# Larger experts: the second pair's down weights fetched into idle scratch instead of the weight ring

## The reference, cut to what matters

```python
def expert_block(args):
    xi, e = args
    hid = jax.nn.silu(xi @ w1[e]) * (xi @ w3[e])
    return hid @ w2[e]
```

## Time and profile before

| | us |
|---|---|
| median of 3 runs | 2576.78 |
| lowest and highest | 2572.59, 2577.24 |
| the profiled execution | 2580.19 |
| its span in the profile | 2578.5 |
| TensorE busy | 2424.8 (94%) |
| VectorE busy | 674.2 (26%) |
| ScalarE busy | 450.8 (17%) |
| DMA | 769.64 MB, mean 298 GB/s |

### The profile page before, as it was taken

One profiled execution on the slowest core, in us unless ns is written; L12 is line 12 of the kernel. 1 busy time (PEld: TensorE's weight loads), 2 busy tenths in 40 slices (PEclk: granted clock), 3 DMA queues, 4 the chain that ended last, 5 costly groups with the idle time before them and its releaser, 6 DMA issues.

```text
span 2578.5 us, 28316 instructions
## 1 busy us (share of the span) xinstructions
PE 2424.8 (94%) x11460; PEld 1388.3 (54%) x11460; DVE 674.2 (26%) x1398; ACT 450.8 (17%) x816; POOL 0.2 (0%) x4
## 2 busy tenths in 40 slices
PE   7999999888888999998888899999999999999998
PEld 5776734333335684433333568884444778874443
DVE  2652331001012223110010244124111633142113
ACT  3141121000001112100000025103111233112111
POOL 0000000000000000000000000000000000000000
PEclk8999999999999899999999999999999999999999
DMA  9348669999998226999999842345999343158994
GB/s 403 139 151 366 269 271 429 429 428 428 429 428 347 98 90 242 428 429 428 428 429 428 349 145 97 126 163 231 420 425 420 142 146 111 66 215 336 428 424 177
DMA packets 53941, 769.64 MB, mean 298 GB/s; under 512 B 5984, under 2 KB 6496, under 8 KB 7008
## 3 DMA queue, kind: packets, MB, share of 16 engines
q1 hardware_dynamic: 53568, 768.17, 72.2%
q10 hardware_dynamic: 288, 0.26, 0.0%
HBM read 767.36 MB, written 1.05 MB: 298 GB/s over the span
## 4 chain that ended last, share of the span: by engine, by line
PE 72%; DMA 24%; DVE 2%; ACT 1%; issue 1%; SPq 0%; ACTq 0%; DVEq 0%
DMA slab<-in_experts 23%; PE psum L400 14%; PE psum L432 13%; PE psum L1933 9%; PE psum L1923 8%; PE psum L1970 7%; PE psum L1905 6%; PE psum L696 4%; PE psum L503 1%; DMA slab<-in_dense 1%; PE psum L1243 1%; PE psum L1956 1%; PE psum L746 1%; PE psum L626 0%; PE psum L1947 0%
## 5 line engine op out<-in xcount | busy, mean ns | idle before, releaser
L1923 PE MATMUL psum<-slab 128*64 128x512 f32 x2048 | 461.5, 597 | 77.1 <-DMA slab<-in_experts 73.8
L400 PE MATMUL psum<-slab 128*128 128x256 f32 (+5 forms) x1464 | 372.3, 412 | 5.2 <-DVE slab L1801 3.4
L1970 PE MATMUL psum<-slab 128*64 128x512 f32 x1536 | 357.8, 601 | 2.6 <-ACT slab L2001 2.6
L1923 PEld LDWEIGHTS psum<-slab 128*64 128x64 f32 x2048 | 142.4, 137 | 389.9 <-issue 273.6
L432 PE MATMUL psum<-slab 128*128 128x256 f32 x1504 | 338.9, 386 | 5.2 <-ACT slab L2158 2.3
L400 PEld LDWEIGHTS psum<-slab 128*128 128x128 f32 (+2 forms) x1464 | 261.8, 189 | 107.5 <-issue 69.1
L432 PEld LDWEIGHTS psum<-slab 128*128 128x128 f32 x1504 | 289.7, 193 | 52.6 <-issue 9.6
L1905 PE MATMUL psum<-slab 128*128 128x256 f32 x1024 | 249.3, 385 | 1.2 <-DVE slab L2023 1.2
L1933 PE MATMUL psum<-slab 128*64 128x512 f32 x1024 | 225.3, 592 | 0.0
L1905 PEld LDWEIGHTS psum<-slab 128*128 128x128 f32 x1024 | 183.2, 189 | 72.7 <-issue 50.3
L2013 DVE TENSOR_TENSOR slab<-psum,slab 128x512 f32<-128x512 f32 (+1 forms) x64 | 35.7, 558 | 691.5 <-PE psum L1923 502.2
(11 more groups left out here) (429 smaller groups left out, 1574.5 us busy)
## 6 DMA issues: line engine op xcount, KB each, us to landing
slab<-in_experts SPq DMA_DIRECT2D x288, 2048.0 KB, 20.2
slab<-in_dense SPq DMA_DIRECT2D x73, 2048.0 KB, 9.4
slab<-in_dense SPq DMA_DIRECT2D x2, 1680.0 KB, 17.9
slab<-in_vec SPq DMA_DIRECT2D x1, 2571.5 KB, 32.8
slab<-in_dense SPq DMA_DIRECT2D x1, 1328.0 KB, 27.4
slab<-in_dense SPq DMA_DIRECT2D x2, 640.0 KB, 14.6
slab<-in_xT SPq DMA_DIRECT2D x1, 1024.0 KB, 8.3
out<-slab SPq DMA_DIRECT2D x2, 512.0 KB, 2.6
```

The lines of the kernel that those rows point to most:

```text
L400: ins = mm(out_ap, lhs, rhs, start=(n == 0), stop=(n == len(pairs) - 1), skip_group_check=True)
L1923: ins = mm(psum[CAP * e:CAP * e + CAP, n, :], xg[:, k, CAP * e:CAP * e + CAP], sl(w, KD)[:, e * (KD // 2) + i, :], start=(k == 0), stop=(k ...
L1970: ins = mm(psum[CAP * e:CAP * e + CAP, 2 + half, :], hidT[:, f, CAP * e:CAP * e + CAP], w, start=(f == 0), stop=(f == fc - 1), skip_group_ ...
```

## The change

The down weights of pair 1, in both layers of the first model, no longer use ring slots. Their 16 blocks go to places in `hT` and the scratch area by five DMAs: three (2048, 2048 and 1536 columns, 11 blocks) are issued right behind the last fill of pass 0, without a wait; two (2048 and 512 columns, 5 blocks, into `order` and the head of `xN`) behind pass 1's four remaining fills and a wait on SP for all eight `sorted_done` of the layer. All five raise `constants_in`. Then pass 2 is issued in straight code, its first two fills into the slots that the first pair's down weights leave, and the loop on SP begins with pass 3. TensorE, ahead of the first down unit of pair 1, waits for `constants_in` in place of a slot, and takes no slot for either half. Units and their numbers are as before.

```diff
+        EARLY_DOWN = ((HO, 0, 0, 2048), (AO + 800 + 13824, 0, 2048, 2048), (AO + 800 + 15872, 1, 2048, 1536),
+                      (AO + 800 + 11776, 1, 0, 2048), (AO + 800 + 4608, 1, 3584, 512))
+
+        def early_down(w0, w1, late):
+
+            return [((w0, w1)[half][:, at:at + n], view(home, n))
+                    for home, half, at, n in (EARLY_DOWN[3:] if late else EARLY_DOWN[:3])]
+
+        def early_block(half, block):
+
+            for home, part, at, n in EARLY_DOWN:
+                if part == half and at <= 512 * block < at + n:
+                    return view(home + 512 * block - at, 512)
...
                 for f, u in zip(pass_fills(l, 0), free):
                     fill(f, first + u)
-                with sp.Fori(1, passes) as i:
+                if kind == 1:
+                    ahead = pass_fills(l, 1)
+                    for src, dst in early_down(ahead[4][0], ahead[5][0], False):
+                        sp.dma_start(dst, src).then_inc(sems["constants_in"], 16)
+                    for f, u in zip(ahead[0:4], free):
+                        fill(f, first + units + u)
+                    sp.wait_ge(sems["sorted_done"], KD * (l + 1))
+                    for src, dst in early_down(ahead[4][0], ahead[5][0], True):
+                        sp.dma_start(dst, src).then_inc(sems["constants_in"], 16)
+                    for f, u in zip(pass_fills(l, 2), free):
+                        fill(f, first + 2 * units + u)
+                with sp.Fori(3 if kind == 1 else 1, passes) as i:
...
             q.e.wait_ge(sems["hidT_ready"], q.due("hidT_ready"))
-            down = slot(q)
+            early = begin and kind == 1
+            if early:
+                q.e.wait_ge(sems["constants_in"], q.due("constants_in", 16 * len(EARLY_DOWN)))
+            down = None if early else slot(q)
             pe_down(kind, down, 0).then_inc(sems["unit_done"], 1)
...
-            if kind == 1:
+            if kind == 1 and not early:
                 down = slot(q)
             pe_down(kind, down, 1).then_inc(sems["unit_done"], 1)
...
-                    w = sl(down, KD)[:, 4 * e + f, :] if kind == 1 else sl(down, 4)[:, 2 * e + f, 512 * half:512 * half + 512]
+                    if down is None:
+                        w = early_block(half, 4 * e + f)
+                    elif kind == 1:
+                        w = sl(down, KD)[:, 4 * e + f, :]
+                    else:
+                        w = sl(down, 4)[:, 2 * e + f, 512 * half:512 * half + 512]
```

More of the change, by code:

```diff
@@ L389, in build @@
         A0 = PER + 288 + 2 * S
+        assert A0 == AO + 800
         def slot(q):
```

## The result

| | before | changed |
|---|---|---|
| median, us (4 runs each) | 2576.27 | 2560.22 |
| lowest, highest | 2572.59, 2577.24 | 2558.62, 2561.34 |
| ratio, 95% interval | | 0.994 (0.9923 to 0.9957) |
| profiled execution, span | 2580.19, 2578.5 | 2561.34, 2559.7 |

The change makes the kernel 16 us faster; 13 were forecast. The spans of the two profiles differ by 18.8 us, so the first question is how much of that belongs to the change.

The account below looks back on a forecast made before the run. Both larger-expert stages were taken as bound by DMA bytes; gains of 6.4 us (layer 0) and 6.5 us (layer 1) sum to 12.9, say 13 us, giving a median of 2563.8 us, range 2557 to 2571 us.

Parts of the forecast that it names:

- What bounds: Larger-expert stages of layers 0 and 1: both end when the bytes have come, with DMA saturated at 428 GB/s.
- ladder: Chain to each stage's end: a DMA piece of 25.5 us, then 16 matmuls of 3.7 us, repeating.
- (2): Ahead of the first pair: 11 early blocks, 2.88 MB, 6.7 us, lie wholly in idle DMA and cost nothing.
- (3): Behind the sort: 5 late blocks, 1.31 MB, 3.1 us, flow in the second idle stretch; the wait costs nothing.
- (4): Down product of pair 1: TensorE's single wait for all 16 blocks has 20 us of slack.
- (5): Start of pass 3, layer 1: full ring makes DMA rest 3.3 us, so pass 3 begins 6.5 us earlier, not 9.8.
- Layer 0: Larger-expert stage of layer 0, by the same steps as layer 1: gain 6.4 us.
- (6): End of both stages: still byte-bound, lead 6.5 us against 52 us deficit; layer 1's last-pair stop of 3.30 us follows.
- rival B: TensorE's stops move with code placement; two more outside byte-bound stretches take 6.6 us: 2570.4 us. Chance of bad case 0.08.
- Rival A: Both layers: the ring does not fill, so the whole 9.8 us per layer is gained: 2557.2 us. Chance 0.05.
- C: Lead does not reach the stages' end, or blocks miss the idle stretches: no difference, 2576.8 us. Chance 0.07.
- D: Pair 1 waits for down weights carried behind pass 2's fills, 15.1 us late: slower by 17.2 us, 2594.0 us. Chance 0.04.

Follow-up runs that it names:

- more scratch: Changed kernel, plus first half of pair 2's down weights moved to the scratch that pair 1's first half leaves: 2560.69 us, then 2560.64 us.

## Why the prediction was right, point by point

- **What bounds** (right). Both stages hang on the bytes: the ladder of landings runs up to the last pair but one in layer 1 in every profile, and up to the last pair in layer 0 in all but one (the second with more scratch, which stopped there). The waits of PE on landings fell: 35.2 us in 32 stops in the earlier trace rows, now 29.1 in 26 over the same stretch.
- **(2) and (3), the early and late blocks cost nothing** (right). They flow in the idle stretches (windows above), and the wait on the sort holds nothing up: pass 2's first fill is issued at 1007.15 us, 0.05 us behind the end of unit 5 (1003.45 + 3.65).
- **(4), no wait at pair 1** (right), and its price if it comes (right: 15.1 us were worked out, 13.7 measured, the whole kernel +18.0 for +17.2).
- **(5), the rest** (right in place and cause, its credit mis-sized). I gave 6.5 us in layer 1; the stage shows 7.5. The term that was mis-sized is the time from the end of a fill's bytes to its landing. I read 2.3 us from a fill deep in a long flow and let it stand for both kernels, so that it dropped out of the difference. SP's issue of pass 3's first fill, before and after, from the views of the two lines:

```profile
L355 SPq DMA_DIRECT2D slab<-in_experts x1: 332/332/332, 1051.7 to 1051.7; - x1
...
DMA to landing us min/median/max: 15.3/15.3/15.3
```

```profile
L380 SPq DMA_DIRECT2D slab<-in_experts x1: 343/343/343, 1040.1 to 1040.1; - x1
...
DMA to landing us min/median/max: 7.7/7.7/7.7
```

The fill landed at 1067.0 us before, as forecast (1060.0 + 4.9 + 2.3 = 1067.2), and at 1047.8 after, 1059.5 in the old frame, where the same lags give 1053.5 + 4.9 + 2.3 = 1060.7. So 7.5 us are won. From the end of unit 13 (1036.27 + 3.6 = 1039.9 us) 7.9 us pass to the landing, not 2.0 + 4.9 + 2.3 = 9.2. The start was as forecast: by the windows from 1041 to 1043 us (262 and 246 GB/s) the flow begins, in effect, at 1041.8 us, 1.9 behind the unit. The missing 1.2 us are in the last term: 1041.8 + 4.9 = 1046.7, landed 1047.8, so 1.1 instead of 2.3 us. The trace of the kernel before could have told me. Its own start from rest, the fill of 1019.0 us:

```profile
L355 SPq DMA_DIRECT2D slab<-in_experts x1: 333/333/333, 1019.0 to 1019.0; - x1
...
DMA to landing us min/median/max: 7.7/7.7/7.7
```

It landed at 1026.7 us, 1.0 behind the end of its bytes (1020.8 + 4.9); the delay of 2.3 us had built up later in the flow, and a rest takes it away.
- **Layer 0** (right in size, in part by luck): 6.4 us forecast, 6.3 measured with the same unit 5. The landing of pass 3's first fill is 7.3 us earlier there too (81.9 us behind the stage's first up product before, 74.6 in the third profile of the changed kernel, which has the same unit 5). So the term was mis-sized here as well; the total came out because a new delay took some 1 us back. By pass 3's fourth fill the lead is 6.5 us (96.6 and 90.1); it lands 5.6 us behind the third there, 6.2 in the first profile, where 4.9 are the bytes.
- **(6), the stop of 3.30 us stays** (right), **rival B** (wrong in its premise): it is there in all twelve profiles of these kernels, 3.1 to 3.9 us, at the end of layer 1's loop, though the code moved; in layer 0 it came once, in the second profile of the kernel with more scratch and not in the first. So where the code lies does not decide it alone: the same kernel showed the stop of layer 0 in one execution and not in the other. What causes it stays open. No further stop came in the changed kernel.
- **Rival A** failed by the rest, seen in the profile; **C** by the ladder; **D** did not occur in the changed kernel, and came true at its price once two DMAs stood later in SP's order.
- **The sum.** Stages 13.9 us for 12.9; the four medians, each beside the kernel before, give 16.1, 16.8, 13.5 and 15.9. The 2 us between are outside the stages and not explained. So the forecast of the median, 3.6 us above what was measured, misses 1 us by the term above, 2 by what lies outside the stages, and 0.5 since the median of before stands at 2576.27 us with its fourth run instead of 2576.78. The profiles' 18.8 holds 3 us more than the medians; the profiled execution of before had 5 us more between the stages than its repeat, of which some 3.4 are the lower clock's by the estimate above. For the same reason layer 1's first pair starts at 973.2 us in the profile and not at the 978 that I gave as a sign.

## What to carry to other kernels

Taking bytes off a saturated queue is worth only what the ring can take up: once all slots are full, the queue rests until TensorE frees the next one. Here six slots filled before TensorE had used one of the next pair, so of 9.8 us per layer 2.3 to 3.5 were given back, and the first half of the blocks had its whole price, the second less than half. Where an early transfer is placed matters only once the ring has room; work out the next full point before looking for more idle time. Read the lag of a landing where the queue has just started and again deep in its flow before using it as one number. And read a stage from its own two marks in several profiles: here a stretch that no edit touched moved by 5 us between two executions, a third of the change.

## What was not expected of the hardware

In a long flow the landings do not keep step with the bytes. In the changed kernel the fill issued at 1018.0 us landed at 1029.4, the next (1021.4) at 1035.8 us, 6.4 us later, and yet the bytes flowed at 431 GB/s from 1011 to 1038 us:

```profile
L351 SPq DMA_DIRECT2D slab<-in_experts x1: 328/328/328, 1018.0 to 1018.0; - x1
...
DMA to landing us min/median/max: 11.4/11.4/11.4
...
L351 SPq DMA_DIRECT2D slab<-in_experts x1: 328/328/328, 1021.4 to 1021.4; - x1
...
DMA to landing us min/median/max: 14.4/14.4/14.4
```

Behind it the flow runs out over 2 us, with shares of 0.12 and 0.04 of 16 engines (about two, then less than one). That reads as one of the 16 engines lagging behind the others while the queue is never empty, every later fill waiting for it, and a rest letting it catch up. It would explain why the rest gave 1 us back. The kernel before shows the same: from rest at 1019.0 us its fill landed after 7.7 us, and the eighth fill behind it landed 1067.0 - 1026.7 = 40.3 us later, where the bytes take 39.2. It is argued from these rows, not shown: no run moved the lag alone. The Trainium skill, DMA: Bandwidth & Descriptors, in the section on why a DMA increments its semaphore by 16, says that the engines of one DMA finish independently and that only the full count means that all has landed; the rows agree with that.
